# Two layers of a hybrid decoder trunk: a norm stage moved from unit 22 to 23, and a turn stage from unit 27 to 26

## What is computed

```
h = rmsnorm(x)
u, sq, sk, sv, dq, dk, dv, gate_logits = split(h @ w_in)
y_ssm = glu(gelu(s5_ssm(u)) @ ssm_w_glu)
y_sb  = stick_breaking_attention(sq, sk, sv)
# differential attention, 4 heads, v of 128, in two blocks of 128 queries
p1 = softmax(mask(q1 k1 * scale));  p2 = softmax(mask(q2 k2 * scale))
o = (p1 - lam * p2) @ v
y_da = rmsnorm(o, subln) * (1 - lam_init)
x += sum(sigmoid(gates) * (branches @ w_branch)) @ w_out
x += cross_attention(rmsnorm(x), mem)
x += square(relu(rmsnorm(x) @ w_up)) @ w_down
```

## Time and profile before

| what | value |
|---|---|
| time before, median of 3 runs | 1017.51 us (1017.29 to 1017.58) |
| the profiled execution's own time | 1019.36 us |
| its span, first to last instruction | 1017.7 us |
| TensorE matmul busy | 979.1 us, 96% |
| TensorE weight loads | 830.1 us, 82% |
| VectorE busy | 749.5 us, 74% |
| ScalarE busy | 566.3 us, 56% |
| GpSimd busy | 46.3 us, 5% |
| mean granted TensorE clock | 0.997 |

### The profile page before, as it was taken

One profiled execution on the slowest core, in us unless ns is written; L12 is line 12 of the kernel. 1 busy time (PEld: TensorE's weight loads), 2 busy tenths in 40 slices (PEclk: granted clock), 3 DMA queues, 4 the chain that ended last, 5 costly groups with the idle time before them and its releaser, 6 DMA issues. The chain is left out here.

```text
span 1017.7 us, 15993 instructions
## 1 busy us (share of the span) xinstructions
PE 979.1 (96%) x5952; PEld 830.1 (82%) x5952; DVE 749.5 (74%) x1161; ACT 566.3 (56%) x867; POOL 46.3 (5%) x104
## 2 busy tenths in 40 slices
PE   6999999999999999999999999999999999999996
PEld 6977777788897888888889777778789878888885
DVE  5988997788765866888765669777887567556665
ACT  7456547675755646444453654657656665444543
POOL 5004000000000004000000110000000000000000
PEclk9999999999999999999999999999999999999999
DMA  8786448455543765686646743564555446665662
GB/s 328 236 195 173 137 132 261 146 171 183 180 135 119 257 195 178 198 226 192 187 130 203 182 147 118 150 194 161 175 177 172 141 130 193 191 186 187 188 189 78
DMA packets 64156, 181.25 MB, mean 178 GB/s; under 512 B 19728, under 2 KB 21776, under 8 KB 63440
## 3 DMA queue, kind: packets, MB, share of 16 engines
q1 hardware_dynamic: 63648, 179.91, 58.4%
q10 hardware_dynamic: 432, 0.32, 0.1%
HBM read 176.67 MB, written 3.54 MB: 177 GB/s over the span
## 5 line engine op out<-in xcount | busy, mean ns | idle before, releaser
L1302 DVE TENSOR_TENSOR s_w_lo<-s_raw,s_w_hi 128x1024 fp32r<-128x1024 f32 x312 | 374.9, 1228 | 104.1 <-ACT s_w_hi L925 100.7
L925 ACT ACTIVATE s_w_hi<-s_raw 128x1024 fp32r<-128x1024 f32 x312 | 321.4, 1056 | 178.6 <-PE p_T L1881 64.5
L1879 PE MATMUL p_A<-s_w_hi,s_bT_hi 128*128 128x512 f32 x352 | 138.2, 393 | 4.5 <-DVE s_bT_lo L1302 2.5
L1881 PE MATMUL p_A<-s_w_hi,s_bT_lo 128*128 128x512 f32 x352 | 137.2, 390 | 0.0
L1880 PE MATMUL p_A<-s_w_lo,s_bT_hi 128*128 128x512 f32 x352 | 137.1, 389 | 0.0
L1879 PE MATMUL p_T<-s_w_hi,s_hT 128*128 128x512 f32 x320 | 128.9, 403 | 5.0 <-ACT s_vN L925 3.3
L1880 PE MATMUL p_T<-s_w_lo,s_hT 128*128 128x512 f32 x320 | 124.9, 390 | 0.0
L1881 PE MATMUL p_T<-s_w_hi,s_hT 128*128 128x512 f32 x320 | 124.9, 390 | 0.0
L1954 PE MATMUL p_T<-s_hT,s_w_hi 128*128 128x512 f32 x256 | 91.3, 399 | 2.1 <-DVE s_hT L1413 2.1
L1954 PE MATMUL p_X<-s_hT,s_w_hi 128*128 128x512 f32 x256 | 91.2, 399 | 0.7 <-ACT s_w_hi L925 0.7
L1879 PEld LDWEIGHTS p_A<-s_w_hi,s_bT_hi 128*128 128x128 f32 x352 | 66.1, 188 | 20.1 <-issue 6.4
(11 more groups left out here) (274 smaller groups left out, 1723.6 us busy)
## 6 DMA issues: line engine op xcount, KB each, us to landing
s_raw<-in_weights SPq DMA_DIRECT2D x312, 512.0 KB, 3.6
s_bt<-in_ssm_bt SPq DMA_DIRECT2D x2, 1024.0 KB, 6.7
s_gates<-f_turn SPq DMA_DIRECT2D x16, 128.0 KB, 6.7
s_x<-in_x SPq DMA_DIRECT2D x1, 1024.0 KB, 10.4
s_dv<-in_ssm_bc SPq DMA_DIRECT2D x2, 512.0 KB, 8.6
u_turn<-s_st_y SPq DMA_DIRECT2D x4, 256.0 KB, 5.0
s_uB<-u_turn SPq DMA_DIRECT2D x16, 64.0 KB, 4.6
s_bt<-in_mem SPq DMA_DIRECT2D x1, 1024.0 KB, 5.9
```

The source lines that it names most:

```text
L925: return nc.scalar.activation(o, i, f, **kw)
L1302: return V.tensor_tensor(o, i0, i1, op)
L1879: mm(o, lhi, rhi, start=first, stop=False, **kw)
L1881: return mm(o, llo, rhi, start=False, stop=last, **kw)
```

## The change

Two numbers in the table of stages change, for both layers:

```diff
     after(21, "da_c", 0)
-    after(22, "da_n", 0)
+    after(23, "da_n", 0)
     after(25, "da_o", 0)
     after(25, "da_c", 1)
     after(25, "da_n", 1)
-    after(27, "da_o", 1)
+    after(26, "da_o", 1)
```

## The result

The changed kernel takes 1020.24 us (median of 9 runs, 1019.81 to 1021.55), the kernel before 1017.51 us (9 runs, 1017.29 to 1019.03). The ratio is 1.0022 with a 95% interval of [1.0014, 1.0031]: 2.7 us slower. The forecast was 1020.4 us.

A forecast was written before the change was run, and what follows sets the result against it. TensorE, busy 96% of the span, was taken as the bound, so only its gaps count. Waits of +1.6 us and one clock fall of +1.3 us gave 2.9 us on the 1017.5 us median: 1020.4 us, range 1018.2 to 1022.2.

The forecast's parts named there:

- The first edit: Norm of the first half moved behind unit 23's other work; unit 26 starts 1.05 us earlier.
- the gap of 1.63 us: TensorE's wait before unit 24 for ScalarE's s_vN; claimed to go, with 0.6 us given back before unit 26.
- The second edit: Turn of the second half moved ahead of unit 27; unit 29 0.8 us late per layer, +1.6 us in both.
- The new gap of 2.95 us: TensorE's wait at the second half's turn, before unit 27, for the second norm's product, ready at 207.65.
- the way of the second product: Chain from ScalarE's evacuations after unit 25 through read-out at 199.06 to the second norm's product, ready at 207.65.
- The one fall in the two layers: TensorE's clock drops behind one new gap of the turn: +1.3 us, chance 0.40.
- No fall: Rival 1: the new wait at the turn without a fall of the clock, 1019.1 us, chance 0.33.
- Two falls: Rival 2: the clock falls behind the turn's gap in both layers, 1021.7 us, chance 0.17.
- The product in time: Rival 3: second norm's product ready without a wait at the turn, 1015.3 us, chance 0.06.
- No change: Rival 4: the 0.95 us gap and other slack swallow everything, between 1017 and 1018 us, chance 0.04.
- the 0.95 us gap: TensorE's wait before unit 29 for VectorE's split s_w_lo; claimed to shrink to near nothing.
- the second rival: The skill's rule at its strictest: the clock falls in both layers, 1021.7 us, chance 0.17.

The follow-up runs named there:

- the version with all gaps filled: Changed kernel plus constant matmuls on TensorE, two in the seam's gap and four in each gap of the turn: 1018.45 us, ratio 1.0003.
- filled, the changed kernel: Changed kernel plus four constant matmuls in each gap of the turn, nothing at the seam: 1018.61 us.
- the pair of filled and unfilled kernels: Second edit alone with four constant matmuls before the second half's turn, 1021.3 us, against the same without them, 1024.43 us.
- the first four kernels: First chip: kernel before again (1017.9 us), first edit alone (1015.47), second edit alone (1024.43), changed kernel again (1020.41); kernel before had median 1017.86.
- the next four: The next four experiments, timed on a second chip beside the kernel before, whose median there was 1017.78 us.
- the last three: The last three experiments, timed on a third chip beside the kernel before, whose median there was 1017.73 us.
- Filling the seam: Changed kernel plus two constant matmuls into idle bank T1 at the seam of the layers: 1020.47 us, ratio 1.0025.

## Why the prediction was right, point by point

**The first edit.** The step in which the gap of 1.63 us goes, 0.6 of it is given back and unit 26 is 1.05 us earlier held in kind, and by size it was pessimistic: the wait is 0.24 us in layer 0, and unit 26 is about 1.2 us earlier. Tested alone, it gives -2.4 us where the chain gave -2.2.

**The second edit.** The new gap of 2.95 us measured 2.54. The mis-sized term is the way of the second product. I added two evacuations of 0.69 us and their handovers, but back to back they take 1.25 us. The trace of before already had such a pair, behind the norm's two instructions:

```profile
186.76 1.25 ACT L925 ACTIVATE s_vN<-p_T,s_stat 128x512 f32<-128x512 f32 x2
```

The read-out came at 198.55 + 0.2 = 198.8 instead of 199.06, and the product followed it, 0.3 us sooner than reckoned. Unit 29 was to be 0.8 us late with both paths meeting there. It was 0.4 us late in layer 0 and 0.6 us in layer 1, and TensorE's own path set it, without a wait. So the 1.6 us for both layers measured 1.0 us by the traces and 0.7 us by the medians (the version with all gaps filled).

**The clock.** The one fall in the two layers, +1.3 us, is what carries the forecast. The gaps of the turn do bring the clock down: filled, the changed kernel goes from a median of 1020.4 to 1018.6 us, and the second edit alone from 1024.43 to 1021.3. The price was too low. I counted 12 matmuls missing from one window at 0.11 us and got 1.3 us. That count takes in matmuls that only reach into the window, so 3.40 / 31 is less than the 0.12 us from one start to the next, and the window misses the first of the slow ones. The seam shows 1.5 us, the turn 1.5 us, the pair of filled and unfilled kernels 1.55 us. The number of falls was luck in part. One was picked among none, one and two with a chance of 0.40, and no row of before could decide it. Most executions of the changed kernel took the time of one fall, some that of two. In the first profile the one fall even sat at the seam, which neither edit touches, and not behind a gap of the turn, where the prediction had put it.

**The sum.** 1.6 + 1.3 = 2.9 was forecast. By the traces it is 1.0 + 1.5 = 2.5 for an execution with one fall. By the medians it is 0.7 + 1.9 = 2.6, with 1020.4 - 1018.5 = 1.9 for the clock. The two ways of dividing it differ by 0.3 us and no run decides between them. The total was closer than its terms, which were wrong in opposite directions. The prediction set its difference against the median although the profiled execution stood 1.85 us above it, and left that surplus out without knowing its cause. The seam's fall is 1.5 us of it, and the median execution of the kernel before doesn't have it.

**The rivals.** No fall (1019.1 forecast) is the filled version: 1018.45. Two falls (1021.7) is what single executions show: 1021.58 has a trace with both, and 1021.55 and 1021.94 have the time. The product in time didn't happen: the waits were 2.5 us, above the 2.15 I gave as the point from which the other side wins. The trace puts that point at 2.54 - 0.4 = 2.1 in layer 0 and 2.52 - 0.6 = 1.9 in layer 1, clock left aside, so it was well placed. "No change" didn't happen either: the 0.95 us gap swallowed a part and not the whole.

**The rule of the Trainium skill** ("TensorE: Matmul & The Clock Gate", "What's actually happening"), that throttled is the default and activity releases it, agrees with these runs. With a gap of 2.76 us in each layer the clock fell behind both in the trace, and matmuls on constants in the gap took the cost away. Taken at its strictest, as in the second rival, it says too much here: with gaps of 2.5 us the median execution has the time of one fall and not of two, and the 1.63 us gaps brought no fall in the traces of the kernel before.

## What to carry to other kernels

A stage that waits must be placed by when its input is ready, not by when its engine is free. The norm, moved behind work that was ready, gave 2.4 us; the turn, moved ahead of work that was ready, took 6.6 us alone. On TensorE such a wait can cost more than its length, because the clock may follow it down: a gap of 2.76 us took 3.3 us from a layer. And one profiled execution can stand on the wrong side of such a fall, so hold its own time against the median before you explain a difference of two microseconds.

## What the runs showed of the hardware that I had not expected

The same program loses the clock in some executions and not in others. At the seam of the kernel before (gaps of 1.32, 0.16 and 0.34 us around eight transpositions) six of 21 executions beside the first four kernels, five of 22 beside the next four and eight of 21 beside the last three took 1.0 to 1.9 us more than the median of the others. In the changed kernel one trace had the fall at the seam alone, one at the seam and behind the second turn, and one, with the seam filled, behind the first turn. Filling the seam left its median where it was (1020.47 us), filling the gaps of the turn brought it to 1018.61 us. What decides in a single execution where the clock falls stays open; no run here moved it on purpose.

Two evacuations of 128 x 512 f32 from PSUM by ScalarE take 1.25 us back to back, in the trace of before (186.76) and after (197.27), where each alone shows 0.69 us.
